# A second block's mixing: three branches by split products, stick-breaking by pairs of heads, the merge by halves

## The reference

```python
u = rms_norm_2(x, mix_norm_g)
q, k, v, cf_val, cf_gate, sc_x, sc_bg, sc_cg, gates = split(u @ w_in)
# stick-breaking attention, 8 heads of 64, strictly causal
z = q_norm @ k_norm.T / sqrt(64)
log_1m_beta = where(causal, -softplus(z), 0)
rest = cumsum(log_1m_beta, reverse=True) - log_1m_beta     # over later keys
attn = where(causal, exp(log_sigmoid(z) + rest), 0)
y_a = (attn @ v) @ w_attn_out                              # "ato"
hb = causal_conv(cf_val * sigmoid(cf_gate), 31 taps) + b
y_b = silu(layer_norm(hb)) @ w_conf_out                    # "cfo"
y_c = (sc_bg * causal_conv(sc_cg * sc_x, 3 taps)) @ w_sc_out   # "sco"
g = sigmoid(gates + gate_b)                                # 3 x 1024
x = x + (g0 * y_a + g1 * y_b + g2 * y_c) @ w_o             # "wf0", "wf1"
x = x + ffn(rms_norm_2(x))                                 # "fi", "fo"
```

## Time and profile before

| | us |
|---|---|
| median of 3 runs (lowest, highest) | 902.26 (900.26, 905.43) |
| the profiled execution's own time | 900.96 |
| its span, first to last instruction | 899.1 |
| PE busy, share of the span | 801.2, 89% |
| DVE busy | 498.9, 55% |
| ACT busy | 380.6, 42% |
| a weight piece from issue to landing, median | 4.8 |
| mean granted TensorE clock | 0.939 |

### The profile page before, as it was taken

The page is one execution under the profiler, slowest core; times in us unless marked ns, Lnnn a source line. Parts: engine busy times, 40 slices in busy tenths (PEclk is TensorE's granted clock), DMA queues, the critical chain, the costliest instruction groups (busy, mean ns, idle before and its releaser), DMA issues.

```text
span 899.1 us, 12063 instructions
## 1 busy us (share of the span) xinstructions
PE 801.2 (89%) x4938; PEld 673.8 (75%) x4938; DVE 498.9 (55%) x718; ACT 380.6 (42%) x584; POOL 26.3 (3%) x40
## 2 busy tenths in 40 slices
PE   4879789967987698778799999999998899999998
PEld 2567566636776576557689999998877699999886
DVE  2365545562683194373756899974552645555541
ACT  3151444560543244361535434449721654444330
POOL 2100001000000000000120000000000000000000
PEclk9789699986998899899899999999999999999999
DMA  9743734463234353320536555553221454455521
GB/s 378 286 170 138 282 119 161 189 243 131 94 134 147 141 187 141 141 102 39 184 113 242 188 183 194 188 181 104 91 94 47 187 188 188 187 185 187 191 94 47
DMA packets 20757, 145.77 MB, mean 162 GB/s; under 512 B 2368, under 2 KB 2528, under 8 KB 3680
## 3 DMA queue, kind: packets, MB, share of 16 engines
q1 hardware_dynamic: 19872, 142.32, 42.5%
q0 software_dynamic: 560, 1.65, 0.7%
q10 hardware_dynamic: 272, 1.05, 0.3%
HBM read 143.95 MB, written 1.05 MB: 161 GB/s over the span
## 4 chain that ended last, share of the span: by engine, by line
PE 49%; DVE 3%; ACT 2%; issue 1%; POOL 0%; DVEq 0%; ACTq 0%
PE banks L404 14%; PE banks L405 14%; PE banks L406 14%; PE banks L453 5%; DVE WL L1436 1%; ACT WH L1012 1%; PE banks L465 1%; PE banks L817 1%; PE banks L842 0%; PE banks L828 0%; ACT ZS L1020 0%; DVE X L1673 0%; ACT ROT L1051 0%; PE banks L830 0%; PE banks L829 0%
## 5 line engine op out<-in xcount | busy, mean ns | idle before, releaser
L1436 DVE TENSOR_TENSOR WL<-RAW,WH 128x2048 fp32r<-128x2048 f32 x101 | 228.4, 2279 | 54.1 <-ACT WH L1012 53.8
L1012 ACT ACTIVATE WH<-RAW 128x2048 fp32r<-128x2048 f32 x101 | 191.2, 1905 | 141.6 <-PE banks L406 78.6
L404 PE MATMUL banks<-HH,WH 128*128 128x256 f32 x768 | 221.6, 289 | 10.8 <-ACT ZS L1067 7.0
L405 PE MATMUL banks<-HL,WH 128*128 128x256 f32 x768 | 220.5, 287 | 0.0
L406 PE MATMUL banks<-HH,WL 128*128 128x256 f32 x768 | 220.2, 287 | 0.0
L404 PE MATMUL banks<-WH,HH 128*128 128x512 f32 (+1 forms) x336 | 140.8, 419 | 36.9 <-DVE WL L1436 19.7
L404 PEld LDWEIGHTS banks<-HH,WH 128*128 128x128 f32 x768 | 151.0, 197 | 12.2 <-issue 7.8
L405 PEld LDWEIGHTS banks<-HL,WH 128*128 128x128 f32 x768 | 151.0, 197 | 0.1
L406 PEld LDWEIGHTS banks<-HH,WL 128*128 128x128 f32 x768 | 150.7, 196 | 0.0
L405 PE MATMUL banks<-WL,HH 128*128 128x512 f32 (+1 forms) x336 | 136.7, 407 | 0.0
L406 PE MATMUL banks<-WH,HL 128*128 128x512 f32 (+1 forms) x336 | 136.0, 405 | 0.0
(11 more groups left out here) (243 smaller groups left out, 854.6 us busy)
## 6 DMA issues: line engine op xcount, KB each, us to landing
RAW<-in_weights_dram SPq DMA_DIRECT2D x130, 1024.0 KB, 4.8
RAW<-in_weights_dram SPq DMA_DIRECT2D x2, 816.0 KB, 7.0
X<-in_x_dram ACTq DMA_DIRECT2D x1, 1024.0 KB, 5.3
QT<-in_weights_dram SPq DMA_DIRECT2D x1, 1024.0 KB, 13.4
V<-in_weights_dram SPq DMA_DIRECT2D x1, 1024.0 KB, 8.4
ZS<-in_weights_dram SPq DMA_DIRECT2D x1, 1024.0 KB, 10.5
out_dram<-X SPq DMA_DIRECT2D x2, 512.0 KB, 2.6
BIG<-in_final_g_dram POOLq DMA_DIRECT2D x1, 512.0 KB, 5.3
```

The costliest lines, as they stand in the source:

```text
L404: pe.matmul(out_, lhsT=w[0], rhs=x[0], start=start, stop=False, **more)
L405: pe.matmul(out_, lhsT=w[0], rhs=x[1], start=False, stop=False, **more)
L1012: do(act.activation(WH[:, s % SPLIT_RING, 0:kb * width], RAW[:, slot[n] % RAW_RING, 0:kb * width], ACT.Copy), high_done)
L1436: do(dve.tensor_tensor(WL[:, s % SPLIT_RING, w], RAW[:, slot[n] % RAW_RING, w], WH[:, s % SPLIT_RING, w], ALU.subtract), low_done)
```

## The change

- **Branches.** sco, cfo and ato become split pieces ("cols"), and wf comes after them. `branch` uses 24 fp32r products for a block, on the high and low parts of its input. ACT and DVE make these parts: SVH, SVL (in the gates), LNYH, LNYL, OSH, OSL.
- **Stick-breaking by pairs.** Scores, rests and weighing take two heads together, interleaved. The mask is added by a fp32r product into the score bank, on the two diagonal squares; the rests are summed into the same bank, and ACT's last Exp reads it there. DVE has one operation a pair left. Pairs take turns in the banks of kind score and of kind turn, so the next pair but one can start when `stick_exp` has drained them. lnT goes to the banks of kind out.
- **Merge by halves.** The merge goes into GT in place. ato.0 waits for OS block by block, and the first half of wf0 and wf1 for tokens 0 to 127 starts when half the merge is done.
- **Order.** The loop is replaced by an order written out, on all three engines. The gates' split of a third piece is moved behind the LayerNorm on DVE, and the pieces from cfo_1 on are split within mixing.

```diff
-    t += rows("wf0", "wf1") + two("sco", 4, 512, "raw") + two("cfo", 4, 512, "raw") + two("ato", 4, 512, "raw")
+    t += two("sco", CB, 512, "cols") + two("cfo", CB, 512, "cols") + two("ato", CB, 512, "cols") + rows("wf0", "wf1")
...
+        PTS = [PT, QR[:, :, 0:TRI]]
+        SVH, SVL, LNYH, LNYL = AL[:, 2:6, :], AH[:, 12:16, :], AH[:, 4:8, :], AL[:, 6:10, :]
+        OSH, OSL = SVH, SVL
...
         def merged_block(j):
-            return QT[:, CB + 2 * j:CB + 2 * j + 2, :] if j < 2 else ZS[:, 2 * j - 4:2 * j - 2, :]
+            return GT[:, 16 + 2 * j:16 + 2 * j + 2, :]
...
+            def branch(name, j, src, ready):
+                wait_parts(pe, name, j // 2)
+                w = parts(name, j // 2)
                 use = f"{name}.{j}"
                 bank = ps.open(pe, "proj", use)
+                if ready:
+                    pe.wait_ge(branch_low, ready)
+                for k in range(CB):
+                    if not ready:
+                        ps.wait_drained(pe, f"so.{k}")
+                    for b in range(2):
+                        f = (2 * (j % 2) + b) * P
+                        mm = product(bank[:, b * S:(b + 1) * S], [part_[:, k, f:f + P] for part_ in w],
+                                     [part_[:, k, :] for part_ in src], k == 0 and b == 0, k == CB - 1 and b == 1)
...
+            def stick_scores(p):
+                pair = (2 * p, 2 * p + 1)
+                banks = [ps.open(pe, ("score", "turn")[p % 2], f"z.{h}") for h in pair]
+                for a, n in ((0, S), (P, P)):
+                    for h, bank in zip(pair, banks):
+                        out_ = bank[:, 0:S] if a == 0 else bank[:, S:TRI]
+                        pe.matmul(out_, lhsT=half_of(h, KT, h // 2, a, a + P), rhs=half_of(h, QT, h // 2, a, a + n),
+                                  start=(a == 0), stop=False)
+                pe.wait_ge(mask_set, 2)
+                for h, bank in zip(pair, banks):
+                    diagonal = bank[:, 0:TRI].rearrange("p (b c) -> p b c", b=3)[:, 0:3:2, :]
+                    mm = pe.matmul(diagonal, lhsT=MASK[:, 0, :], rhs=MASK[:, 1, :].unsqueeze(1).to_broadcast([P, 2, P]),
+                                   start=False, stop=True)
+                    ps.fill(mm, f"z.{h}")
+            def stick_rest(p):
+                pe.wait_ge(soft_masked, p + 1)
+                for h in (2 * p, 2 * p + 1):
+                    bank = tiles[ps.uses[f"z.{h}"][0]]
...
+            def stick_weigh(p):
+                pair = (2 * p, 2 * p + 1)
+                bank = ps.open(pe, "out", f"so.{p}")
+                for h in pair:
+                    ps.wait_drained(pe, f"z.{h}")
...
+            stick_scores(1)
+            conv(0)
             pe.wait_ge(late_got, 16)
+            stick_rest(0)
+            norm_back()
+            conv(1)
+            stick_scores(2)
+            conv(2)
+            stick_rest(1)
+            conv(3)
             for t in range(NT):
+                ps.wait_drained(pe, f"v2.{t}")
+            stick_weigh(0)
+            stick_scores(3)
+            conf(0)
+            stick_rest(2)
+            stick_weigh(1)
+            conf(1)
+            conf(2)
+            stick_rest(3)
+            stick_weigh(2)
+            conf(3)
+            stick_weigh(3)
             for j in range(4):
+                branch("ato", j, (OSH, OSL), 0)
+            for c in range(2):
+                pe.wait_ge(mt_low, 2)
+                half_tokens(f"wf{c}", 0, 0, use=f"y2.0.{c}")
             pe.wait_ge(mt_low, 4)
             output(2)
...
+            def soft(p):                                   # ACT
...
+                do(act.activation(b, twins[stick_twin(p)][:, :, 0:TRI], ACT.Abs))
+                do(act.activation(b, b, ACT.Exp, scale=-1.0))
+                do(act.activation(b, b, ACT.Ln, bias=1.0), soft_ln)
+            def stick_exp(p):
+                if p >= 2:
+                    ps.wait_filled(act, f"so.{p - 2}")
+                for h in (2 * p, 2 * p + 1):
+                    act.wait_ge(rest_sum, h + 1)
+                    bank = tiles[ps.uses[f"z.{h}"][0]]
+                    ps.drain(act.activation(PTS[p % 2][:, h % 2, :], bank[:, 0:TRI], ACT.Exp), f"z.{h}")
...
+                    if (g, j) == (5, 0):                   # in ACT's loop over the gates
+                        soft(0)
+            highs(branch_first + 4)
+            soft(1)
+            stick_exp(0)
...
+            for t in range(NT):                            # behind the eviction of lnT
+                high_conf(t)
+            soft(2)
+            highs(branch_first + 5)
+            stick_exp(1)
+            soft(3)
+            high_stick(0)
+            highs(branch_first + 6)
+            stick_exp(2)
+            high_stick(1)
+            highs(branch_first + 7)
+            stick_exp(3)
+            high_stick(2)
+            highs(branch_first + 8)
+            high_stick(3)
             for j in range(4):
                 act.wait_ge(merged, j + 1)
                 do(act.activation(HH[:, 2 * j:2 * j + 2, :], merged_block(j), ACT.Copy), mt_high)
+                if j == 2:
+                    highs(branch_first + 9)
+            highs(branch_first + 10)
...
+            def soft(p):                                   # DVE
+                dve.wait_ge(soft_ln, p + 1)
+                do(dve.scalar_tensor_tensor(b, twins[stick_twin(p)][:, :, 0:TRI], 0.0, b, ALU.max, ALU.add), soft_masked)
...
+            soft(0)
+            lows(branch_first + 4)
+            soft(1)
+            conv(0)
+            conv(1)
...
+            conv(2)
+            soft(2)
+            conv(3)
+            lows(branch_first + 5)
+            soft(3)
+            conf(0)
+            low_stick(0)
+            lows(branch_first + 6)
+            conf(1)
+            low_stick(1)
+            lows(branch_first + 7)
+            conf(2)
+            low_stick(2)
+            conf(3)
+            lows(branch_first + 8)
+            low_stick(3)
             for j in range(4):
                 branch(f"ato.{j}", j, 0, False, True)
                 low_merged(j)
+            lows(branch_first + 10)
```

More of the change, by code:

```diff
@@ L868, in _, with norm_back @@
-            for o in range(4):
-                ps.wait_drained(pe, f"so.{o}")
+            def norm_back():
+                for t in range(NT):
+                    ps.wait_drained(pe, f"ln.{t}")
+                    turn(f"lnT.{t}", [LNH[:, t, b * P:(b + 1) * P] for b in range(CB)], kind="out")
+            conv = lambda j: branch("sco", j, (SVH, SVL), 2)
+            conf = lambda j: branch("cfo", j, (LNYH, LNYL), 4)
+            stick_scores(1)
+            conv(0)
+            pe.wait_ge(late_got, 16)
@@ L1888, in _, with low_conv, low_conf, low_stick @@
                 ps.drain(dve.tensor_tensor(sv, bank[:, :].rearrange("p (b s) -> p b s", b=2), sv, ALU.mult), f"sbg.{j}")
-            for n in range(12):
+            def low_conv(j):
+                dve.wait_ge(branch_high, j + 1)
+                sv = SV[:, 2 * j:2 * j + 2, :]
+                do(dve.tensor_tensor(SVL[:, 2 * j:2 * j + 2, :], sv, SVH[:, 2 * j:2 * j + 2, :], ALU.subtract), branch_low)
+            def low_conf(t):
+                dve.wait_ge(branch_high, 2 + t + 1)
+                span = slice(t * P, (t + 1) * P)
+                do(dve.tensor_tensor(LNYL[:, :, span], LNY[:, :, span], LNYH[:, :, span], ALU.subtract), branch_low)
+            def low_stick(p):
+                dve.wait_ge(branch_high, 4 + p + 1)
+                bank = ps.wait_filled(dve, f"so.{p}")
+                ps.drain(dve.tensor_tensor(OSL[:, p, :], bank[:, 0:S], OSH[:, p, :], ALU.subtract), f"so.{p}")
+            branch_first = first_split("sco")
+            for n in range(11):
                 feed(f"g{n // 2}", n % 2)
+                if n == 4:
+                    low_conv(0)
+                    low_conv(1)
                 conf_taps(min(12 + 2 * n, CONF_TAPS), min(14 + 2 * n, CONF_TAPS))
@@ L1939, in add_rest @@
-            def add_rest(h):
-                bank = ps.wait_filled(dve, f"r.{h}")
-                ps.wait_drained(dve, f"z.{h}")
-                p = PR[:, h % 3, :]
-                ps.drain(dve.tensor_tensor(p, bank[:, 0:TRI], p, ALU.add), f"r.{h}")
-            for i in range(S_HEADS + 5):
-                if i < S_HEADS:
-                    soft_mask(i)
-                if 0 <= i - 2 < S_HEADS:
-                    add_rest(i - 2)
-                if i < 4:
-                    branch(f"sco.{i}", i, 16, True)
-                elif i < 8:
-                    branch(f"cfo.{i - 4}", i - 4, 8, False)
-                if 0 <= i - 5 < S_HEADS and (i - 5) % 2:
-                    o = (i - 5) // 2
-                    bank = ps.wait_filled(dve, f"so.{o}")
-                    ps.drain(dve.tensor_copy(OS[:, o, :], bank[:, 0:S]), f"so.{o}")
+            conv = lambda j: branch(f"sco.{j}", j, 16, True)
@@ new lines, in _ @@
+            conf = lambda j: branch(f"cfo.{j}", j, 8, False)
```

(11 more changed lines are left out.)

181 lines of the change are left out of this document (67 added, 114 removed).

## The result

Four runs of the changed kernel have a median of 890.41 us (886.04 to 891.82), against 903.51 for the kernel before (four runs): a ratio of 0.987, 95% interval 0.9838 to 0.9902. Forecast were 894.5 us, a range of 887 to 900, and "faster by more than 0.5%" at 0.81. The direction and the range held. The gain was 1.3% where 0.9% was forecast (13.1 us between the medians), and where the difference came from is the matter of what follows.

A forecast was written before the change was run, and what follows sets the result against it. TensorE was taken to bound mixing. 17 us gained (products 13, first wait and clock 1.28 + 1.9, small waits about 1) less 10 given back left 7.4: 894.5 us forecast, 8 in 10 from 887 to 900.

The forecast's parts named there:

- products 13: TensorE in mixing: split branch blocks, paired scores and paired products with V relieve it of 12 to 13 us.
- The wait at scores(3): Fourth pair's scores: TensorE waits 4.0 us for banks that ScalarE's stick_exp(1) drains late, then 1.6 lost to the clock.
- The wait of 0.7 at scores(2): Third pair's scores: TensorE waits 0.7 us for the banks that stick_exp(0) drains.
- The end: End of mixing: waits of 2.0 us at ato.0 for OSL and 2.75 before wf1's first half, the old 2.89 moved.
- 10 given back: TensorE in mixing: waits of 0.7, 4.0 and 2.0 us and two new slow spells of 1.6 reduce the gain.
- each wait over 1.2 us in this part cost clock: TensorE in mixing: a wait of 1.3 to 2.9 us is followed by some 3.3 at half clock, costing 1.6 to 1.9.
- (b): Rival for the clock and ScalarE: the clock stays high or ScalarE keeps up, 10 to 16 us gained; chance 0.22.
- (a): The forecast's own case: ScalarE's queue gives back half, 5 to 10 us gained; chance 0.60.
- (c): Rival for mixing: waits and clock eat nearly all of the gain, 0 to 4.5 us left; chance 0.12.
- (d): Rival: the clock falls at scores(3) and stays low through mixing, slower by over 0.5%, about 925 us throughout; chance 0.06.
- the drain at each table load: Rival on ScalarE: each table load holds it another 1.38 us, so no gain at all; chance 0.02, within the 0.12.
- LayerNorm: VectorE takes the statistics ahead of a split: TensorE's wait for LNH and its slow spell go, 1.28 + 1.9 us.

The follow-up runs named there:

- plain: Changed kernel with each branch block as eight plain f32 products; stretch (ScalarE's Tanh of g5.0 to VectorE's adding of y2.0.1) 82.31 us against 79.44.
- serial: Changed kernel with a pair's two heads one after the other in the score products and the products with V; stretch 80.23 us against 79.44.
- apart: serial with each head's mask product right behind its own scores, so it stands between the two heads; stretch 81.51 us, changed kernel 79.44.
- expfirst: Changed kernel with stick_exp(1) moved ahead of soft(2) and the splitting of ato_0 in ScalarE's queue; stretch 72.95 us against 79.44.
- noload: Changed kernel with Tanh in place of Ln in soft, so no function table is loaded in the stretch (output wrong); stretch 72.87 us against 79.44.
- nohalf: Changed kernel without the early halves of wf, TensorE waiting for the whole merge; stretch 80.97 us against 79.44.
- before_ln: Kernel before, with only the split ahead of the LayerNorm statistics on VectorE moved behind them; stretch 89.60 us against 91.15.
- again: Changed kernel run once more, unaltered, beside best; stretch 77.87 us, ratio to the kernel before 0.9906.
- tail: Changed kernel with the last pair's high and low parts ahead of splitting wf0_1, and wf1_0 split behind the second merged block; stretch 78.17 us against 79.44.
- all: Changed kernel with the orders of expfirst and tail together; stretch 74.25 us, ratio to the kernel before 0.9807.
- best: expfirst plus the last pair's parts ahead of splitting wf0_1, and wf1_0 split behind the third merged block; stretch 72.20 us, ratio to the kernel before 0.9812.

## Why the prediction was right, and where its size came from

- **The bound.** TensorE's work was the bound of mixing, and the change relieved it. The stretch without waits and spells is 91.15 - 5.4 (1.28, 2.89, and about 1.2 of small waits, most of it behind the last heads) - 3.4 for spells, 82.4 before, and 79.44 - 7.7 - 3.4, 68.3 after. The term "products 13" measured 14. A block was 2.81 where it stands between a mask product and a sum, and 2.97 or 2.98 behind the turns (614.02 to 617.00) and ahead of the products with V (2.98 forecast for all), and the sums of a pair 1.75 (611.48 to 613.23) where 1.94 was carried over. plain shows the part of the branches, 8.0. The other 6.1 is pairs and sums; of it no run prices the products with V by themselves.
- **Pairs.** Scores with mask 1.19 us (607.48 to 608.67), forecast 1.16; the mask pair 0.34. serial and apart show that the heads' standing next to each other, not their interleaving, is what saves.
- **The wait at scores(3)**, the largest term of what is given back: 3.41 for 4.0, for the named cause. expfirst and noload remove it in two ways. The wait of 0.7 at scores(2) did not come: stick_exp(0) ended at 616.55, before TensorE had finished conv(1) (617.00).
- **The end.** 1.57 for 2.0 and 2.78 for 2.75. nohalf bears out that the old wait is moved and not removed: taking the early halves out costs 0.4 of wait, and 1.2 of a longer spell.
- **The step that was mis-sized** is "10 given back": waits 0.7, 4.0 and 2.0 and two new slow spells of 1.6. Measured were waits of 3.41 and 1.57 and one new spell of 1.7, 6.7 in all. I charged a spell at ato.0 by the rule "each wait over 1.2 us in this part cost clock", drawn from two cases. That rule was wrong: the seven waits of 1.56 or 1.57 us had no spell behind them. That, 1.7 of shorter waits and 1 of products are the 4.3 us between 7.4 and 11.7.
- **Rivals.** (b), "10 to 16 us gained", was given 0.22 and is what the stretch shows (11.7), while the mechanism was that of (a): ScalarE's queue gives back part, but 6.7 us where it had 10. In the profiled executions the whole time fell by 9.5 us, within (a)'s 10, and in the second pair of medians by 9.3; in the first pair it fell by 13.1. So the chances of 0.60 and 0.22 are not settled by whole runs. (c) and (d) fell, and with (c) the drain at each table load.
- **LayerNorm.** 3.2 us were booked for it, with 1.9 for the spell, which cost 1.7; before_ln confirms wait and spell, and shows that the same edit in the old order gives 1.5 back at once.
- **VectorE and transfers** were costed at nothing in the middle; no wait of TensorE names them there.

What stays open: whether low_conv in the gates costs anything was not tried by itself (no wait of TensorE in the gates names it), and why the same wait of 2.8 us is followed by a spell in one execution and not in another.

## What to carry to other kernels

Lay out the queue of each engine by hand with durations from the trace: here it foretold, before any run, at which products three waits would stand and their lengths to within 0.6 us each. When an engine is almost always busy and another waits for it, ask first for the order of its queue: one line moved was worth some 5 us (3.4 of wait, 1.7 of clock; 6.5 against one execution of the changed kernel, 4.9 against the other), more than all that was tried around the end. Price a wait of TensorE with and without the clock behind it, and measure a change on its own stretch, since the rest of the program can scatter by more than the change is worth.

## What was not expected of the hardware

- **Which wait costs clock.** In the stretch no spell follows a wait of 1.57 us (changed, serial, nohalf, expfirst, noload, again, apart). Every wait of 3.14 to 3.41 us has one (changed, serial, nohalf, tail, all, again), and so have 2.45 (plain) and 2.13 (best). Waits of 2.75 to 2.9 have one in before, changed, serial, before_ln and apart, and not in expfirst, noload and again. But waits of 1.28 (before) and 1.32 (apart) were followed by one, and one of 1.46 (before_ln) was not. Behind the stretch a wait of 3.34 (noload) and one of 3.37 (serial) had none. The length of the wait alone does not settle it. The lines of noload:

```profile
685.48 0.47 PE L410 MATMUL banks<-WH,HH 128*128 128x512 f32 x1 [3.34 <-DVE WL L1508]
```

```profile
684.00:690.00 6.00, 4.52 (x20) 3.79 (x21) 3.83 (x5) 4.09 (x4) 0.55 (x1) 1.00 0.91 348
690.00:700.00 10.00, 8.56 (x43) 6.97 (x42) 6.56 (x10) 5.02 (x10) 0.00 (x0) 1.00 0.56 212
```

- **When the spell begins, and how long it is.** In the changed kernel TensorE goes on at 629.92, and the clock falls only at 631.4; in apart it goes on at 630.45, and the clock falls at 633.1. In serial, nohalf and all the clock fell 1.2 to 1.3 us before the wait was over, and there the spell is 6.8 us long. In the stretch all others, which began behind the wait or at most 0.5 us before its end, are 3.4 us.
- **Two heads of 64 rows run together in any order** if the mask product does not stand between them: 0.86 us for both, 0.85 for one.
- **A common start that scatters.** The Tanh of g5.0 lies between 594.5 and 605.4 us in kernels that are the same up to there.
